# Twenty up-projection blocks as seven products of sums, their modulation sums on TensorE, and the last expert matrix split by columns

## The reference, cut to what matters

```python
# first block, layer l; x and ctx go through the same weights
mod_x = silu_c @ w_mod[l] + b_mod[l]           # 6 x 1024 numbers: shifts, scales, gates
mod_c = silu_cc @ w_mod[l] + b_mod[l]
...
x = layer_norm(ALPHA * x + g2 * squared_relu_mlp(modulate(x, sh2, sc2), w_up[l], w_down[l]), ...)
def squared_relu_mlp(h, w_up, w_down):         # w_up: 1024 x 4096
    return jnp.square(jax.nn.relu(h @ w_up)) @ w_down
# second block: 16 experts, 32 tokens each
hid = silu(xs @ w1) * (xs @ w3)
ys = (hid @ w2) * gate                         # added back to the chosen tokens, then x + g2 * that
```

## Time and profile before

| | before |
|---|---|
| median of runs | 3002.67 us |
| profiled execution, its own time | 3002.67 us |
| its span | 3000.9 us |
| PE busy | 2664.2 us (89%) |
| PE weight loads (PEld, beside PE) | 1647.5 us (55%) |
| DVE busy | 1328.7 us (44%) |
| ACT busy | 489.1 us (16%) |

### The profile page before, as it was taken

The page is one execution under the profiler, slowest core; times in us unless marked ns, Lnnn a source line. Parts: engine busy times, 40 slices in busy tenths (PEclk is TensorE's granted clock), DMA queues, the critical chain, the costliest instruction groups (busy, mean ns, idle before and its releaser), DMA issues. The chain is left out here.

```text
span 3000.9 us, 44859 instructions
## 1 busy us (share of the span) xinstructions
PE 2664.2 (89%) x19732; PEld 1647.5 (55%) x19732; DVE 1328.7 (44%) x2505; ACT 489.1 (16%) x1155; POOL 26.4 (1%) x48
## 2 busy tenths in 40 slices
PE   6999999999998999998999988889989889766655
PEld 3467844446867888734753333345448687433323
DVE  2775388542474776586421111131476763100001
ACT  1023200000213000224321111011051311100000
POOL 0000000000000000000000000000000000000000
PEclk9999999999999999998999999999999999987878
DMA  9530255342251577221149999992110017899998
GB/s 360 196 140 13 92 205 211 154 168 112 96 213 69 222 283 280 72 77 40 59 173 402 428 428 427 428 403 53 36 45 30 2 37 307 362 427 427 427 427 353
DMA packets 67874, 651.27 MB, mean 217 GB/s; under 512 B 14944, under 2 KB 26848, under 8 KB 28000
## 3 DMA queue, kind: packets, MB, share of 16 engines
q1 hardware_dynamic: 67680, 648.41, 53.4%
HBM read 644.06 MB, written 4.33 MB: 216 GB/s over the span
## 5 line engine op out<-in xcount | busy, mean ns | idle before, releaser
L376 PE MATMUL ps<-HT,ring 128*128 128x256 f32 (+1 forms) x3152 | 904.9, 445 | 6.4 <-DMA ring<-in_w_in 1.6
L376 PEld LDWEIGHTS ps<-HT,ring 128*128 128x128 f32 x3152 | 589.7, 190 | 283.6 <-issue 225.6
L2454 PE MATMUL ps<-ring,arena 128*32 128x256 f32 (+1 forms) x2944 | 370.2, 505 | 111.3 <-DMA ring<-in_moe_w 101.9
L478 DVE SCALAR_TENSOR_TENSOR acc<-ring,sil,acc 128x512 f32<-128x512 f32 x616 | 411.8, 747 | 0.0
L376 PE MATMUL ps<-arena,ring 128*128 128x256 f32 (+3 forms) x1232 | 373.6, 464 | 3.4 <-PEq L719 2.2
L2454 PEld LDWEIGHTS ps<-ring,arena 128*32 128x32 f32 (+1 forms) x2944 | 140.1, 130 | 317.5 <-issue 196.1
L376 PEld LDWEIGHTS ps<-arena,ring 128*128 128x128 f32 (+2 forms) x1232 | 230.3, 188 | 139.1 <-issue 119.2
L1053 DVE SCALAR_TENSOR_TENSOR XT<-ps,modcols,XT 128x256 f32<-128x256 f32 x124 | 55.8, 481 | 274.4 <-PE ps L376 140.4
L2475 PE MATMUL ps<-ring,conv 128*64 128x512 f32 x496 | 112.3, 596 | 24.2 <-DMA ring<-in_moe_w 23.6
L2475 PE MATMUL ps<-ring,arena 128*32 128x256 f32 x960 | 80.6, 494 | 57.6 <-DMA ring<-in_moe_w 57.1
L496 ACT ACTIVATE modrows<-ps 128x128 f32<-128x128 f32 x44 | 12.2, 277 | 574.8 <-PE ps L492 574.8
(11 more groups left out here) (432 smaller groups left out, 2594.0 us busy)
## 6 DMA issues: line engine op xcount, KB each, us to landing
ring<-in_moe_w SPq DMA_DIRECT2D x184, 2048.0 KB, 25.6
ring<-in_w_mod SPq DMA_DIRECT2D x24, 2048.0 KB, 8.0
ring<-in_ada_w SPq DMA_DIRECT2D x24, 2048.0 KB, 8.0
ring<-in_w_up SPq DMA_DIRECT2D x16, 2048.0 KB, 12.1
ring<-in_w_down SPq DMA_DIRECT2D x16, 2048.0 KB, 12.2
ring<-in_w_in SPq DMA_DIRECT2D x10, 2048.0 KB, 10.2
ring<-in_od_w_in SPq DMA_DIRECT2D x6, 2048.0 KB, 25.6
arena<-in_moe_w SPq DMA_DIRECT2D x10, 1024.0 KB, 20.6
```

Of the source, the lines that this page charges most:

```text
L376: last = nc.tensor.matmul(bank_of(job, j), lhsT, rhs, start=n == 0, stop=n == len(terms) - 1)
L478: ins = nc.vector.scalar_tensor_tensor(out=acc, in0=weights[:, k, :], scalar=s, in1=acc, op0=ALU.mult, op1=ALU.add)
L2454: last = nc.tensor.matmul(K.ps[M * j:M * j + M, 2 * (e % 2) + i, 0:FW], xs[:, e // 4 % 2, e % 4, 4 * h + k, :], weights((m, e, h), k, slic ...
```

## The change

Four parts.

1. The 20 up-projection blocks 8 to 27 are taken in ten pairs. For a pair, the two weight blocks a and b, each split in two by the contracted features, and the two token segments, each split in the same way, form a 2 x 2 product of blocks. Eight products of half size would do it; the new code does it with seven products of sums and differences (Winograd's form). DVE forms four combinations of the tokens once and four of the weights for each pair. PE's order is P of pair g, C of g-1, A of g, D of g-1, B of g; P, C and A are four matmuls of 256 columns, D and B eight. DVE adds the products in PSUM to partial results in SBUF, ACT copies P and applies Relu and Square to the finished pair. Blocks 28 to 31 stay as they were.
2. `woven` takes the place of `filled` in this stage: behind each job it puts either the sum of a modulation piece on PE (`modulation_sums`, like the first stage's) or the turn of the piece summed before. All twelve pieces are summed so. The order has 0, 0, 2, 3, 3, 3, 1, 0 modulation pieces behind the eight up pieces. A job may name its PSUM bank. The constant tables are overwritten by token sums and loaded again in the down-projection.
3. The last expert's w2 is laid out in two halves by columns. The first half is multiplied, copied, scattered and added before the second; only half of the scatter, additions and stores is left behind the last piece.
4. The root spreads of `QueryKeyNorm` start one job later.

The core of the diff ("..." where lines are left out):

```diff
+BY_COLUMNS = (DEPTH - 1, "moe_w2", NE - 1)
-    counts = {... "up0": (0, 2, 2, 2, 2, 2, 2, 0), ...
+    counts = {... "up0": (0, 0, 2, 3, 3, 3, 1, 0), ...
+def modulation_sums(K, layer, piece):
+    nc, vectors = K.nc, K.sil[:, layer // 2]
+    def build(ps, slots):
+        for k in range(KD):
+            for j in range(4):
+                last = nc.tensor.matmul(ps[32 * j:32 * j + 32, :], vectors[:, k, :], slots[0][:, k, j * P:(j + 1) * P], start=k == 0, stop=k == KD - 1)
+        return last
+    return dict(pieces=[piece], rows=(0, P), n=P, only="act", build=build, bank=4,
+                evac=lambda side, ps, eng: nc.scalar.activation(K.modrows[:, :], ps, ACT.Copy))
+def woven(K, order, dense, jobs, shift, summed):
...
+    for job in dense:
+        p = job["pieces"][0]
+        while pairs and where[pairs[0]] < where[p] + 3:
+            queue.append(pairs.pop(0))
+        job = job | dict(pieces=[where[p]])
...
+        job["place"](len(jobs))
+        jobs.append(job)
+        if turning:
+            jobs.append(modulation_columns(K, *turning) | dict(bank=5))
+            turning = None
...
+        elif [x for x in queue if x in summed]:
+            turned = [x for x in queue if x in summed][0]
+            queue.remove(turned)
+            jobs.append(modulation_sums(K, turned[0], where[turned]))
+            turning = (*turned, len(jobs) - 1)
+class TokenSums:
...
+        tt(self.t1, self.h12, self.h11, ALU.subtract).then_inc(*K.inc("tokens_combined"))
+        tt(self.t3, self.h22, self.h12, ALU.subtract).then_inc(*K.inc("tokens_combined"))
...
+        tt(self.t2, self.h22, self.t1, ALU.subtract).then_inc(*K.inc("tokens_combined"))
...
+        tt(self.t4, self.h21, self.t2, ALU.subtract).then_inc(*K.inc("tokens_combined"))
+class SevenProducts:
...
+    def differ(self, dve):
...
+        dve.wait_ge(*K.landed(self.first + self.at["slot"]))
+        tt(self.s3, a11, a21, ALU.subtract).then_inc(*K.inc("weights_combined"))
+        tt(a21, a21, a22, ALU.add).then_inc(*K.inc("weights_combined"))
+    def combine(self, dve):
...
+        tt(self.s2, a21, a11, ALU.subtract).then_inc(*K.inc("weights_combined"))
...
+        tt(self.s4, a12, self.s2, ALU.subtract).then_inc(*K.inc("weights_combined"))
+    def multiply(self, ps, weights, tokens):
+        for k in range(4):
+            last = self.K.nc.tensor.matmul(ps, weights[:, k, :], tokens[:, k, :], start=k == 0, stop=k == 3)
+        return last
+    def plain(self, pe, ps, w):                      # P
+        return self.multiply(ps[:, 0:T], self.blocks(w)[0], self.t.h11)
+    def upper(self, pe, ps, w):                      # A
...
+        return self.multiply(ps[:, T:TT], self.s2, self.t.t2)
+    def middle(self, pe, ps, w):                     # B
+        self.multiply(ps[:, 0:T], self.blocks(w)[2], self.t.t1)
+        return self.multiply(ps[:, T:TT], self.s3, self.t.t3)
+    def finish_upper(self, pe, ps, w):               # C
+        return self.multiply(ps[:, 0:T], self.blocks(w)[1], self.t.h21)
+    def finish_middle(self, pe, ps, w):              # D
...
+        self.multiply(ps[:, 0:T], self.s4, self.t.h22)
+        return self.multiply(ps[:, T:TT], self.blocks(w)[3], self.t.t4)
...
 def out_and_up_stage(K, l, heads):
...
-    dense = [feature_job(K, fb // 4, ... evac=squared_relu(K, hidden[:, fb, :])) for fb in range(8, 32)]
-    jobs = filled(K, order, dense, jobs, 2)
+    for g in range(11):
...
+            dense.append(group.job("P", group.plain, group.keep_plain, "act", g % 2))
...
+            dense.append(before.job("C", before.finish_upper, before.keep_first, "dve", (g - 1) % 2, room=1) ...
+            dense.append(group.job("A", group.upper, group.keep_common, "dve", g % 2, room=1))
...
+            dense.append(before.job("D", before.finish_middle, before.keep_rest, "dve", 2 + (g - 1) % 2, room=2))
...
+            dense.append(group.job("B", group.middle, group.keep_lower, "dve", 2 + g % 2, room=1) ...
+    woven(K, order, dense, jobs, 2, modulation_of(1, range(12)))
...
-    gemm_stage(K, n + len(order), jobs, "down_and_in", before=times_alpha(K, TT), **extra)
+    gemm_stage(K, n + len(order), jobs, "down_and_in", before=times_alpha(K, TT),
+               also=K.constants(["swap1", "cos1", "sin1", "cn", "sn", "cm", "sm"], K.arena[:, 16512:18432]), **extra)
...
+            def down_columns(h):
...
+                        last = nc.tensor.matmul(K.ps[M * j:M * j + M, 5 - h, 0:P], hidT[:, c, M * f:M * f + M], w[:, k, j * P:(j + 1) * P],
+                                                start=k == 0, stop=k == KD - 1)
...
+            if halved:
...
+                down_columns(0)
+                pe.wait_ge(*K.at("ys_kept", 2 * NE))
+                scatter_last(0, 4)
+                down_columns(1)
+                pe.wait_ge(*K.at("ys_kept", 2 * NE + 2))
...
-        return [((j, 0), self.add_up)] + [((j + 2 + i, 0), lambda pe, i=i: self.spread(pe, i)) for i in range(6)]
+        return [((j, 0), self.add_up)] + [((j + 3 + i, 0), lambda pe, i=i: self.spread(pe, i)) for i in range(6)]
```

More of the change, by code:

```diff
@@ L313, in gemm_stage @@
     turn = [sides[:j + 1].count(sides[j]) for j in range(len(jobs))]
+    bank = [job.get("bank", j % banks) for j, job in enumerate(jobs)]
+    last_in_bank = [max((i for i in range(j) if bank[i] == bank[j]), default=None) for j in range(len(jobs))]
     def bank_of(job, j):
         p0, p1 = job["rows"]
-        return K.ps[p0:p1, j % banks, 0:job["n"]]
+        return K.ps[p0:p1, bank[j], 0:job["n"]]
     def emit_steps(pe, j, n):
@@ L389, in _ @@
                     last = job["build"](bank_of(job, j), [K.slot(first + i) for i in pieces])
+                elif "products" in job:
+                    for i in pieces:
+                        await_piece(i)
+                    last = job["products"](pe, bank_of(job, j), [K.slot(first + i) for i in pieces][0])
                 elif "emit" in job:
-                    last = job["emit"](j % banks)
+                    last = job["emit"](bank[j])
                 else:
@@ L457, in token_job, with accumulation @@
         evac=lambda side, ps, eng: evacuate(K, side, out, ps))
-def accumulation(K, vectors, piece, done, free):
+def accumulation(K, vectors, piece, done, free, k0=0, k1=KD):
     nc, first = K.nc, K.cursor
@@ L470, in work @@
         weights = K.slot(first + piece)
-        for k in range(KD):
+        for k in range(k0, k1):
             for v in range(2):
@@ L513, in modulation_columns @@
                 build=lambda ps, slots: nc.tensor.transpose(ps, K.modrows[:, :], K.ident))
+def modulation_sums(K, layer, piece):
[8 more added lines that the diff above has]
+def woven(K, order, dense, jobs, shift, summed):
+    where = {p: shift + n for n, p in enumerate(order)}
+    queue, running, turning, step, done, free = [], None, None, 0, 0, None
+    pairs = [p for p in order if isinstance(p, tuple)]
+    arrived = 0
+    for job in dense:
[3 more added lines that the diff above has]
+        job = job | dict(pieces=[where[p]])
+        if running is None and [x for x in queue if x not in summed]:
+            running, step = [x for x in queue if x not in summed][0], 0
+            queue.remove(running)
+        if running and job.get("room"):
+            upto = min(KD, step + job["room"])
+            job["accumulate"] = accumulation(K, K.sil[:, running[0] // 2], where[running], done, free, step, upto)
+            step = upto
+        job["place"](len(jobs))
[3 more added lines that the diff above has]
+            turning = None
+        elif running and step == KD:
+            done += 2 * KD
+            free = len(jobs)
+            jobs.append(modulation_rows(K, where[running], done) | dict(bank=4))
+            running, turning = None, (*running, free)
+        elif [x for x in queue if x in summed]:
[3 more added lines that the diff above has]
+            turning = (*turned, len(jobs) - 1)
+    assert not queue and not pairs and running is None and turning is None, (queue, pairs, running, turning)
+    return jobs
 def filled(K, order, dense, jobs=None, shift=0, state=None):
@@ L1450, in out_and_routing_stage, with evicted, __init__, make @@
     gemm_stage(K, 2, jobs, "out_projection", ahead=ahead, banks=SUMS, tail=routing, **beside)
+def evicted(K, jobs, j):
+    sides = [job.get("only") or ("act", "dve")[i % 2] for i, job in enumerate(jobs[:j + 1])]
+    return K.at(sides[j] + "_evacuated", sides.count(sides[j]))
+class TokenSums:
+    def __init__(self, K, tiles):
+        self.K = K
+        self.h11, self.h12, self.h21, self.h22 = (K.HT[:, 4 * i:4 * i + 4, SEGS[s]] for i in range(2) for s in range(2))
+        self.t1, self.t2, self.t3, self.t4 = (a.rearrange("p (k t) -> p k t", k=4) for a in tiles)
+    def make(self, dve):
+        K, tt = self.K, self.K.nc.vector.tensor_tensor
+        tt(self.t1, self.h12, self.h11, ALU.subtract).then_inc(*K.inc("tokens_combined"))
```

(40 more changed lines are left out.)

120 lines of the change are left out of this document (104 added, 16 removed).

## The result

The changed kernel takes 3015.22 us (median of four runs, 3014.39 to 3016.14) against 3003.32 for the kernel before in the same comparison. The ratio is 1.0044, 95% interval [1.0031, 1.0057]: 11.9 us slower, where the prediction had 8.0. The profiled execution took 3014.39 us, its span is 3012.6.

The account below looks back on a forecast made before the run. TensorE bounds the up-projection, transfers the expert loops. The stage's 174.7 + 8.2 + 3.0 + 1.7 = 187.6 against 176.4 gives +11.2, less 3.2 at the end: 3002.67 + 8.0 = 3010.7 us, range 3001 to 3016.

Parts of the forecast that it names:

- the price of the low clock: Up-projection, behind each late modulation sum: TensorE runs at a lower clock, 1.5 us a wait, 3.0 us together.
- the two waits: Up-projection, behind B4 and B6: TensorE waits for late modulation pieces M13 and M17, 4.1 us each, 8.2 us together.
- the sign of the sum: Whole kernel: all terms added up to a slower kernel, +8.0 us.
- PE's work: Up-projection stage: TensorE's own instructions take 174.7 us; seven products save 17.5, the modulation sums cost 15.8 more.
- the bound of 9.0: Up-projection: most that both waits together could cost, if a load takes 8.0 us, the page's median.
- The upper bound: Up-projection, low clock behind a wait: at most 1.95 us a wait, all of a sum at half the clock.
- Last matrix: Kernel's end, last expert's w2 by columns: 3.2 us shorter, between 3.4 and 2.1 with the low clock.
- The other edits: Down-projection constant reloads cost nothing, at worst 3.2 us; root spreads one job later cost 0.
- (a): Up-projection: the clock does not fall behind the waits; +5.0 us, 3007.7 us in total; chance 0.17.
- (b): Up-projection: the two waits do not appear; -3.2 us, 2999.5 us in total; chance 0.15.
- (c): Up-projection: TensorE waits at A for s2 or P's copy, 0.5 us a group, 3015.7 us in total; chance 0.18.
- own range: Whole kernel: 3007 to 3014 us for the main forecast alone, chance 0.50; two fifths counted as slower.

## Why the prediction was partly wrong

The step that failed is the price of the low clock behind the two waits: the prediction let it end with the sum that had waited, 1.5 us a wait, and it ran on over the next product, 2.5 us a wait. The waits themselves were also taken a little short. The mechanisms that lengthen the stage were right, and so was the sign of the sum; but most of the chance went to a change too small to tell, where the run is clearly slower.

**PE's work: right.** Forecast 174.7 us and 1.7 for the end. Measured: 190.5 less 9.0 for the waits, 5.0 for the clock and 1.6 for the end (the idle time at 561.11) leaves 174.9. The cost of the sums was 15.7 (15.8 forecast). The products gained 15.9 between whole stages, where the forecast is 17.5 less 1.7 for the new end, 15.8.

**The two waits: right in place, a little short.** Forecast 4.1 each, behind B4 and B6; measured 4.55 and 4.45. For the first of them the load goes out 0.20 us after D3, not 0.1, lands 7.9 after its issue, not 7.6, and can be used 8.08 after it, not 7.7; PE's own work between was 3.73. That is 0.20 + 8.08 - 3.73 = 4.55. I had taken the lowest landing of the earlier trace rows, 7.6; the median there, 8.0, gave the bound of 9.0 for the two, which is what came.

**The clock: the step that failed.** The prediction took 1.5 us a wait, from the one sum of the earlier trace rows. Measured: each sum lost 3.57 - 1.89 = 1.68, and the product behind it another 0.88 and 0.73 over its 1.83. That is 5.0 together, not 3.0. The granted clock is 0.50 from 443.70 to 448.50, over the sum's end, and 0.81 to 450.0; I had priced the sum and ended the low clock with it. The upper bound, all of one sum at half the clock, was no bound either, for the same reason. In the earlier trace rows the sum at 24.27 is shorter (3.40) and ran beside a column of 1.00; here duration and column agree. The Trainium skill ("TensorE: Matmul & The Clock Gate", HAM oscillation) tells of tiles that start at the lower clock after each wait for a transfer; this trace agrees, twice in twelve sums, and with unused matmuls in the wait neither is slow. The sum at 24.27 in the kernel before had next to nothing right behind it, so its row could not show the rest of the price. The next block in that timeline could have warned, though it had a wait of its own:

```profile
30.01 8.80 PE L376 MATMUL ps<-HT,ring 128*128 128x512 f32 x16 [1.60 <-DMA ring<-in_w_in]
```

Its 16 records take 8.80 us where a block of the earlier trace rows takes 7.13, and the clock reads 0.67 from 30.0 to 32.0 and 0.50 to 34.0.

**Last matrix: the size right, one sign not.** 3.2 forecast, 3.6 measured. The matmuls take 1.95, and the first of the last additions comes 3.40 us after the last piece's first matmul, 4.90 before: 1.5 earlier, as forecast. From that addition to the end are 4.3 us, 6.45 before: 2.1 less, where four stores fewer were priced at 1.9. But it is not so that only half of the stores is left behind the last piece: all eight go out from 3007.03 on, 0.20 after its last matmul, since SP waits for the release of every piece before it stores. The first four go out beside the copies and the scatter, so that four follow the addition, and the price held.

**The other edits: right.** The seven constants took 3.38 us of SP at 561.07, and its next ring load, whose turn came at 589.45, was 28 us away. The first root spread, now at 2131.32, follows PE's work without idling.

**The rivals.** (a) and (b) fell: the clock did fall, and both waits stood. (c) fell, though its total of 3015.7 was the nearest; a right number from a wrong mechanism. Added up, the sum's misses are 0.8 for the waits, 2.0 for the clock, 0.2 of work less 0.1 at the end, -0.4 at the last matrix, and 1.2 us in the stretches that were not touched (0.5 and 0.9, less the 0.2 by which the old stage began ahead of SP's issue of the earlier trace rows): 3.7, of the 3.9 between 8.0 and 11.9 (the rest lies between one execution and the medians). The 1.2 is no mechanism of the change that I can name: single stages differ by up to 3.2 us either way. And as 8.0 stood one microsecond under what can be told from no change, with two rivals below it, misses of 2.8 for clock and waits were enough. Of the own range of 3007 to 3014 a third, not two fifths, lies above 3011.7, which changes little.

## What to carry to other kernels

Where an engine that sets the time is made to do work for one that doesn't, price the exchange first: here seven products saved what the sums cost, and sharing the sums between both engines took 5.6 us off the stage. An order of loads has to be followed to the slot's last user: a load that goes out one job before its use leaves PE idle, and the idle time is paid a second time in the clock behind it. Price that second part by all work that runs until the clock is back, not by the first instruction.

## What the runs showed of the hardware

Behind idle times of 4.55 and 4.45 us the granted clock was 0.50 for some 5 us in which PE was busy throughout; in the run with unused matmuls, behind 0.61 and 0.86 us of idleness, sums and products had their usual durations. Four loads issued within 1.5 us of each other (435.6 to 437) hardly held up the first: it landed 7.9 us after its issue, near the 7.6 of a lone one, and the last of them after 22.1. And 256-column products with weight loads of 0.19 us ran as fast a column as 512-column ones (0.432 us a matmul against 0.859), ten groups long.
